# Attention steps moved into the transposed projections of a hybrid attention block, with the small projections rearranged

## The reference

```
h = RMSNorm(x) * ln_g
qa ka va za | qb ckv iq ik iw zb | qc kc vc zc | ga gb gc = columns of h @ w_in
A: 16 heads, 2 key heads, window of 2 chunks of 64, sinks, T5 bias
B: ckv = RMSNorm(ckv); score = sum_h iw_h relu(iq_h . ik) ; best 64 keys per query;
   attention over them with keys ckv @ w_uk and values ckv @ w_uv, T5 bias
C: 16 heads over all earlier chunks, relative bias
y_b = mixer_b * silu(z_b);  merged = sum_b sigmoid(g_b) * (y_b @ w_p_b)
out = RMSNorm(x + merged @ w_o) * final_g
```

## Time and profile before

| | |
|---|---|
| time, median of 3 runs | 977.41 us (976.91 to 977.55) |
| the profiled execution's own time | 976.46 us |
| its span | 974.6 us |
| PE busy | 965.2 us (99%) |
| DVE busy | 606.9 us (62%) |
| ACT busy | 473.7 us (49%) |
| granted clock of PE, mean | 0.998 |
| DMA | 190.34 MB, mean 195 GB/s |

### The profile page before, as it was taken

How to read it: one execution, slowest core, us unless ns; L and a number is a source line. 1 busy time by engine, 2 the same in 40 slices (tenths; PEclk the granted TensorE clock), 3 DMA queues, 4 the chain that set the end, 5 groups by cost and what they waited for, 6 DMA issues and landing times.

```text
span 974.6 us, 13317 instructions
## 1 busy us (share of the span) xinstructions
PE 965.2 (99%) x5136; PEld 814.8 (84%) x5136; DVE 606.9 (62%) x1129; ACT 473.7 (49%) x785; POOL 27.6 (3%) x28
## 2 busy tenths in 40 slices
PE   9999999999999999999999999999999999999996
PEld 7888888888888888888888888888888888888885
DVE  7585655676675756586765555766655555555563
ACT  7553444555453545463553544644534444444442
POOL 0030000000000110010000000000000000000000
PEclk9999999999999999999999999999999999999999
DMA  9853645465554655554654745646455677565553
GB/s 337 294 187 119 233 170 193 154 222 177 204 193 142 233 176 184 197 205 141 243 186 148 253 155 191 208 152 225 163 191 181 198 294 227 180 189 187 176 176 126
DMA packets 54766, 190.34 MB, mean 195 GB/s; under 512 B 6192, under 2 KB 7088, under 8 KB 54064
## 3 DMA queue, kind: packets, MB, share of 16 engines
q1 hardware_dynamic: 54416, 189.23, 57.1%
q10 hardware_dynamic: 288, 0.27, 0.1%
HBM read 187.38 MB, written 2.10 MB: 194 GB/s over the span
## 4 chain that ended last, share of the span: by engine, by line
PE 98%; DMA 1%; SPq 0%; ACT 0%; DVE 0%; issue 0%; ACTq 0%; POOLq 0%; POOL 0%
PE bank L1015 24%; PE bank L1005 19%; PE bank L1007 19%; PE bank L1006 19%; PE bank L1018 12%; PE bank L981 2%; PE bank L1051 2%; PE bank L1071 2%; DMA raw<-in_w_s_dram 1%; PE bank L1188 0%; PE bank L1146 0%; PE bank L1147 0%; PE bank L1145 0%; DVE w_lo L634 0%; ACT w_hi L446 0%; SPq L367 0%
## 5 line engine op out<-in xcount | busy, mean ns | idle before, releaser
L634 DVE TENSOR_TENSOR w_lo<-raw,w_hi 128x1024 fp32r<-128x1024 f32 (+1 forms) x326 | 388.0, 1213 | 174.0 <-ACT w_hi L446 173.1
L446 ACT ACTIVATE w_hi<-raw 128x1024 fp32r<-128x1024 f32 (+1 forms) x326 | 334.8, 1046 | 299.5 <-PE bank L1007 206.0
L1015 PE MATMUL bank<-hT,w_hi 128*128 128x512 f32 x960 | 300.9, 397 | 0.0
L1007 PE MATMUL bank<-w_hi,hT 128*128 128x512 f32 x600 | 233.6, 389 | 0.0
L1018 PEld LDWEIGHTS bank<-hT,w_lo 128*128 128x128 f32 x960 | 178.1, 188 | 41.1
L1005 PE MATMUL bank<-w_hi,hT 128*128 128x512 f32 x504 | 197.2, 391 | 0.0
L1006 PE MATMUL bank<-w_lo,hT 128*128 128x512 f32 x504 | 196.1, 389 | 0.0
L1018 PE MATMUL bank<-hT,w_lo 128*128 128x256 f32 x960 | 186.3, 278 | 0.0
L1015 PEld LDWEIGHTS bank<-hT,w_hi 128*128 128x128 f32 x960 | 147.6, 189 | 3.4
L1007 PEld LDWEIGHTS bank<-w_hi,hT 128*128 128x128 f32 x600 | 112.8, 188 | 23.6
L1005 PE MATMUL bank<-w_hi,ybuf 128*128 128x512 f32 x296 | 116.7, 394 | 0.2 <-DVE w_lo L634 0.2
(11 more groups left out here) (152 smaller groups left out, 534.6 us busy)
## 6 DMA issues: line engine op xcount, KB each, us to landing
raw<-in_w_s_dram SPq DMA_DIRECT2D x320, 512.0 KB, 4.4
bias_t<-in_bias_dram SPq DMA_DIRECT2D x24, 384.0 KB, 3.1
raw<-in_w_s_dram SPq DMA_DIRECT2D x8, 256.0 KB, 4.2
merged<-in_x_dram SPq DMA_DIRECT2D x2, 1024.0 KB, 9.8
big<-in_x_dram SPq DMA_DIRECT2D x1, 2048.0 KB, 9.6
out_dram<-big SPq DMA_DIRECT2D x8, 256.0 KB, 2.7
big<-in_x_t_dram SPq DMA_DIRECT2D x7, 256.0 KB, 6.7
k_b<-in_final_g_dram SPq DMA_DIRECT2D x1, 1024.0 KB, 11.6
```

The lines of the kernel that those rows point to most:

```text
L446: nc.scalar.activation(halves(g)[0], raw[:, s, 0:n], ACT.Copy).then_inc(hi_ready, 1)
L634: nc.vector.tensor_tensor(low, raw[:, s, 0:n], high.bitcast(F32), ALU.subtract).then_inc(lo_ready, 1)
L1007: ins = mm(acc, xl, wh[:, e, :], start=False, stop=kt == n_kt - 1)
L1015: mm(bank[2 * (c % 2) + n][:, :], wh[:, e, n * P:(n + 1) * P], hl_t[:, kt, :, :], start=kt == 0, stop=False)
```

## The change

The order of chunks, the slots and the lags:

```
-CHUNKS = ([("kvc", 0, 0), ("v", 0, 0), ("v", 0, 1), ("iq", 0, 0), ("ik", 0, 0)] + quarters("q", 0) + quarters("z", 0)
+CHUNKS = ([("kvc", 0, 0), ("v", 0, 0), ("v", 0, 1), ("iq", 0, 0), ("ka", 0, 0)] + quarters("q", 0)
           + [k for u in range(4) for k in (("q", 1, u), ("uk", 0, u))]
           + [("q", 2, 0), ("uv", 0, 0), ("q", 2, 1), ("uv", 0, 1), ("q", 2, 2), ("q", 2, 3)]
-          + quarters("k", 0) + quarters("z", 1)
-          + branch(0) + quarters("z", 2) + branch(1) + branch(2) + quarters("o", 0))
+          + quarters("k", 0) + quarters("z", 0) + quarters("z", 1) + quarters("z", 2)
+          + branch(0) + branch(1) + branch(2) + quarters("o", 0))
+KW = 456
+IDX_AT = (3, 6)
 def slots():
-    ...
+    for i in range(-1, 7):
+        yield i, FIRST[AT["q", 1, 0]] + 2 + 5 * (i + 1)
+    for i in range(7, 24):
+        yield i, FIRST[AT["k", 0, 0]] + 4 + (7 * (i - 7) + 1) // 2
-                bias_at[SLOT_G[2 * (p // 2) - 3] + 5 + p % 2] = p
+                bias_at[SLOT_G[2 * (p // 2) - 3] + 6 + p % 2] = p
 # ACT, attend:
+                    elif q >= 0:
+                        sc.wait_ge(pv_ready, q + 1)
+                        sc.wait_ge(scored, min(q + 2, NPAIR // 2))
+                        for p in (2 * q, 2 * q + 1):
+                            for t in range(NT):
+                                nc.scalar.activation(qT[p // 8][:, p % 8, P * t:P * (t + 1)],
+                                                     bank[4 + 2 * (p % 2) + t][:, SROW:CH], ACT.Copy, scale=0.25
+                                                     ).then_inc(o_ready, 1)
-                    p = scored_at(g - 3 - e) + e        # exponentials
+                    p = scored_at(g - 2 - e) + e
 # DVE, attend: the four products by silu are gone
-                    p = scored_at(g - 2 - e) + e        # bias and maximum
+                    p = scored_at(g - 1 - e) + e
+                        if p > 1:
+                            ve.wait_ge(o_ready, 2 * p - 2)
-                    p = scored_at(g - 4 - e) + e        # scaling
+                    p = scored_at(g - 3 - e) + e
 # DVE, silu_chunk, at the end:
+                ve.wait_ge(dve_evac, dves_before(c + 1))
+                ve.wait_ge(o_ready, 4 * (4 * b + u + 1))
+                for half in range(2):
+                    m = 2 * u + half
+                    nc.vector.tensor_tensor(qT[b][:, m, :], qT[b][:, m, :], silu[:, half, :], ALU.mult
+                                            ).then_inc(y_ready, 1)
-            rounds = {("z", 0, 0): 0, ("z", 0, 1): 1, ("z", 0, 2): 2, ("z", 0, 3): 3, ("q", 1, 1): 4, ("q", 1, 3): 5,
-                      ("q", 2, 1): 6, ("q", 2, 3): 7}
+            rounds = {("q", b, u): 4 * b + u - 4 for b in (1, 2) for u in range(4)}
```

More of the change, by code:

```diff
@@ L84, in dves_before @@
 def dves_before(c):
[L86 removed]
+    return sum(k in COPIED + SUMMED + ("iq", "z", "P") for k in KINDS[:c])
 def sums_before(c):
[L91 removed]
+    return sum(BLOCKS.get(k, 0) for k in KINDS[:c])
 def tanhs_before(c):
@@ L607, in _ @@
                     sc.wait_ge(dve_evac, dves_before(c))
-                    for n in range(4 if kind == "iq" else 2):
+                    for n in range(BLOCKS[kind]):
                         carry(c, n, HD ** -0.5 if kind == "q" else 1.0)
@@ L936, in _ @@
                         transpose_lo(7)
-                if kind == "ik":
-                    ve.wait_ge(used, FIRST[c + 1])
-                    for r in (slice(0, HD), slice(HD, P)):
-                        nc.vector.tensor_copy(ikT[r, :], bank[0][0:HD, 0:SEQ])
-                    nc.vector.tensor_copy(iwT, bank[0][HD:HD + IH, 0:SEQ]).then_inc(dve_evac, 1)
+                if kind == "ka":
+                    ve.wait_ge(carried, sums_before(c) + 1)
+                    for group in range(2):
+                        src = slice(HD * group, HD * (group + 1))
+                        for dst in (slice(0, HD), slice(HD, P)):
+                            ins = nc.vector.tensor_tensor(kT_a[dst, group, :], bank[0][src, 0:SEQ],
+                                                          gate[src, 0, SEQ:CH], ALU.add)
+                    ins.then_inc(dve_evac, 1)
                 if kind in ("v", "uv"):
                     copy_chunk(c)
-                if kind in SUMMED + ("iq",):
+                if kind in ("q", "k", "uk") + ("iq",):
                     sum_chunk(c)
@@ L999, in rows_step @@
             def rows_step(g, c, e, kt, n_kt, hi_t, lo_t, ts=range(NT)):
-                wh, wl = parts(g, CH)
+                cols = KW if KINDS[c] == "kvc" else CH
+                wh, wl = parts(g, cols)
                 for t in ts:
                     xh, xl = hi_t[:, kt, t * P:(t + 1) * P], lo_t[:, kt, t * P:(t + 1) * P]
-                    acc = bank[2 * (c % 2) + t][:, :]
+                    acc = bank[2 * (c % 2) + t][:, 0:cols]
                     mm(acc, xh, wh[:, e, :], start=kt == 0, stop=False)
@@ L1138, in _ @@
                             ins.then_inc(ckvT_ready, 1)
-                    elif kind == "ik":
-                        pe.wait_ge(lo_ready, g + 1)
-                        wh, wl = (w[:, g % RING, 0:288].rearrange("p (k n) -> p k n", k=4) for w in (w_hi, w_lo))
-                        acc = bank[2 * (c % 2)][0:72, 0:SEQ]
-                        for e in range(4):
-                            kt = 4 * j + e
-                            mm(acc, wh[:, e, :], h_hi[:, kt, :], start=kt == 0, stop=False)
-                            mm(acc, wh[:, e, :], h_lo[:, kt, :], start=False, stop=False)
-                            ins = mm(acc, wl[:, e, :], h_hi[:, kt, :], start=False, stop=kt == KT - 1)
-                        ins.then_inc(used, 1)
+                            pe.wait_ge(act_evac, 1)
+                            pe.wait_ge(dve_evac, 1)
+                            for t in range(NT):
+                                ins = transpose(bank[6][:, t * P:(t + 1) * P], ik[:, t, :])
+                            ins.then_inc(ikT_ready, 1)
                     elif kind == "uk":
```

168 lines of the change are left out of this document (66 added, 102 removed).

## The result

The changed kernel takes 1003.34 us (median of 4 runs, 1000.59 to 1006.39), beside 977.16 for the one before on the same chip: 1.027 times as long, 95% interval 1.0249 to 1.029. That is 26 us slower, and 2.3 us beyond the top of the range. The waits came as forecast; a term for TensorE's clock was missing from the sum. Its profiled execution took 1006.39 with a span of 1004.6, so it is the longest of the four.

The account below looks back on a forecast made before the run. TensorE's list bounds the kernel (99% busy). Span 974.6 - 3.3 (list) - 0.1 (end) + 15.3 (waits) + 6.4 (masks) + 1.0 (early slots) = 993.9, plus 1.9 around it: 995.8, about 995.5 us; range 986 to 1001.

Parts of the forecast that it names:

- rival 3: Long waits let TensorE's clock down behind waits of 3.1 and 5.3 us, some 1.5 each at least: 999 us, chance 0.1.
- The waits: Odd to even slots, four pieces instead of six: TensorE waits for scaled probabilities, 15.3 us over eight intervals before masks.
- S + 13.8: S is the first product behind slot 19; the walk through helper lists ends slot 20's scaling 13.8 us later, wait 2.7.
- DVE's own list: Between slots 15 and 16, VectorE's list sets the chain at 14.0 us, a wait of 2.9.
- The masks: POOL's bias masks behind slots 7, 9 and 11 hold VectorE's low parts, small sums and new product: 6.4 us, between 0 and 12.
- The list and the head: TensorE's shorter kvc, transposes and index scores save 3.3 us, between 2.6 and 4; head's wait at the eleventh piece taken as 0.
- The end: Behind the last sum, one small operation goes from POOL to DVE and the scaling is split: 0.1 us less.
- The early slots: Slots -1 and 1, five pieces to the next with uk between: waits of 0.5 us each, 1.0; slots 3 and 5 none.
- Rival 1: The waits do not come, since the lists run more closely than the walk: 973.1 us, faster; chance 0.12.
- Rival 2: The waits come, but masks fall on VectorE's idle time: 989.4 us; chance 0.2.
- Rival 4: VectorE falls behind in low parts, so pieces wait half a microsecond at each of twelve z chunks: 1001 us; chance 0.05.
- Rival 5: Waits so short that they eat the 3.4 us gained: 977 us; chance 0.03.

Follow-up runs that it names:

- filled: Changed kernel with matmuls that serve nothing ahead of the waits of seven even slots, keeping TensorE busy: 996.6 us, ratio 1.0201.
- half filled: Changed kernel with half as many matmuls that serve nothing ahead of those seven waits (7, 5, 15, 7, 7, 7, 7): 996.32 us, ratio 1.0204.
- The two shortened kernels: Changed kernel with ScalarE's carries and tanh ending z chunks, or VectorE's new product, cut from 256 to 16 columns: 1001.77 and 1000.47 us.
- VectorE's product short: Changed kernel with VectorE's new product at the end of a z chunk cut from 256 to 16 columns: 1000.47 us, one execution.
- second profile of the changed kernel: Changed kernel run again with nothing edited, for a second profile and more times: 1003.68 us, ratio 1.0272.
- measured alone: Kernel before, its order, slots and lags kept, with the changed kernel's small projections, transposes, index scores and end: 973.51 us, ratio 0.9965.
- nine profiles: Profiles of the small projections alone, the changed kernel and seven more with the same head: first transposed product began between 70.62 and 72.26.
- the last kernel: Changed kernel, odd-to-even slots six pieces apart early, five from slot 7, six between 11 and 12, two behind 12; x rows later: 973.72 us.

## Why the prediction was wrong in size and right in kind

**The step that failed is the half clock.** The sum went to 995.8 with no term for it. It stood as rival 3, with a chance of 0.1, a price of 3 us, and the sentence "Waits of 3.1 and 5.3 us reach that". That sentence took a bound from the earlier trace rows, where the clock fell some 3 us behind the last matmul, and read it as if shorter waits were safe. The runs show otherwise: waits of 2.0 to 2.8 us were followed by 1.2 GHz at slots 8, 10, 20 and 22 of the first profile. So seven waits could draw it, not two, and five did. The term is 6.7 us (1003.3 against 996.6 filled, and 996.3 half filled) where the forecast had none and the rival 3. With it the sum is 1002.5, above the range. The sum also started from the profiled execution's 976.46; the median of the kernel before is 977.16 beside the changed one, 0.7 more. The chance was wrong too: one row of a clock that falls within the length of my own waits should have put the term into the sum, or the top of the range above 1001.

**The waits.** Right: 22.7 forecast, 21.2 of idle time and 23.2 by starts; the kernels in which they are filled take 996.6 and 996.3, where the sum without clock said 995.8. Slot 18 with none, slot 12 longest, and all released by the scaling came as written. For slot 20 the walk said S + 13.8; S is 449.23 here and the scaling ended at 462.33 + 1.01 = 463.34, S + 14.1:

```profile
449.23 0.73 PE L1020 MATMUL bank<-hT,w_hi 128*128 128x512 f32 x2
```

```profile
462.33 1.01 DVE L686 TENSOR_SCALAR scores<-scores,r_denom 128x256 f32<-128x256 f32 x4
```

The two shortened kernels show whose list sets them: ScalarE's at slots 14, 20 and 22, with VectorE's product on the path of slot 20 by 0.14. Slot 16 was right as "DVE's own list", but by 0.2 only. The gap of 2.3 us or more that I had named as a sign was missed at slot 10 (2.03).

**The masks.** Forecast 6.4 (1.5, 2.3, 2.6); measured 1.1, 2.0 and 2.7, 5.7. At slot 12 POOL and VectorE of the changed kernel show the hold in both directions:

```profile
353.13 2.75 POOL L424 TENSOR_TENSOR bias_t<-bias_t,chosen 128x768 f32<-128x768 f32 x1 [5.85 <-DMA bias_t<-in_bias_dram]
```

```profile
353.00 1.23 DVE L633 TENSOR_TENSOR w_lo<-raw,w_hi 128x1024 fp32r<-128x1024 f32 x1 [0.31 <-ACT w_hi L441]
354.14 1.76 DVE L678 TENSOR_TENSOR denom<-expsum,sink_exp 128x4 f32<-128x4 f32 x1
```

The mask began inside a low part and took 2.75 instead of 1.85, while the low part kept its 1.23; the small sum behind it then took 1.76 instead of 0.15. So the mask waited for the low part, and the sum for the mask: the case that no row of before had shown. With VectorE's product short it went the other way at the first mask of this slot: in the changed kernel it had held the product (2.42 instead of 0.76 at 345.15), and now it held the low part behind it, which took 2.71 instead of 1.22:

```profile
343.27 1.85 POOL L424 TENSOR_TENSOR bias_t<-bias_t,chosen 128x768 f32<-128x768 f32 x1 [23.35 <-DMA bias_t<-in_bias_dram]
```

```profile
343.49 2.71 DVE L633 TENSOR_TENSOR w_lo<-raw,w_hi 128x1024 fp32r<-128x1024 f32 x1 [0.21 <-ACT w_hi L441]
```

The Trainium skill's rule (SBUF — State Buffer, Who interferes with whom), that whoever starts first has the shared ports to its end, agrees with these rows.

What I listed as held was incomplete. In front of slot 10 the two masks held a small sum and a scaling (L686), which reads one tile and no bank and took 2.41 instead of 1.01:

```profile
318.42 1.81 DVE L678 TENSOR_TENSOR denom<-expsum,sink_exp 128x4 f32<-128x4 f32 x1
...
320.48 2.41 DVE L686 TENSOR_SCALAR scores<-scores,r_denom 128x256 f32<-128x256 f32 x4
```

Both are on the path: VectorE has no idle time from there to the scaling that releases slot 10. Together they were held by 3.06. In the second profile of the changed kernel a low part (2.76 instead of 1.22) and the scaling (2.32) were held, by 2.85 together, and slot 10 idled 0.22 less. That the forecast of 2.3 came near is in part luck: my walk let everything on VectorE wait for the mask's end, whatever the operation.

**The list and the head.** Right in sum, 3.4 forecast and 3.36 measured alone (976.87 - 973.51). Inside it, kvc's matmuls came 0.207 apart, not 0.202: 1.9 instead of 2.4. So the other terms must have brought some 0.5 more than I gave them; no run separates them. The taking of 0 for the head's wait was 1.5 off in the profiled execution and about 0.3 off on average over nine profiles.

**The end.** 0.1 forecast, 0.1 measured. **The early slots.** 0.5 each forecast, 0.4 and 0.36 by starts.

**Behind the slots.** From the first gate product (514.41) to the last matmul (996.56) the 176 pieces took 482.2, or 2.74 each, as six of them did in 16.46 before: nothing changed there, as forecast.

**Rivals 1, 2, 4 and 5** are refuted: the waits came, the masks cost 5.7, and the only wait for a low part between slots 6 and 22 is one of 0.34. (Rival 4's twelve half microseconds on 995.8 make 1001.8, not 1001.)

## What to carry to other kernels

When an order is changed, measure the distance between two steps that depend on each other against the list that the slowest helper engine must work off between them, interval by interval; here one piece more per interval gave back 26 us with the same work in the same places. Put into the sum, and not among the rivals, what a wait does to the clock behind it: here waits of 2.0 us and more on TensorE were in some executions followed by a stretch at 1.2 GHz that lost 1.5 to 3.0 us, and it comes in one execution and not in the next, so the range has to be wide on that side. And evening out a sequence by one place can put a copy behind another engine's long item, so look at both neighbours of the interval that is widened.

## What the runs showed of the hardware that was not expected

- Equal waits, unequal clock: 2.79 us at slot 16 was followed by 1.00 in one profile (transposes 1.53) and by 0.50 in the next (2.82). Over the profiles, waits of 1.31 to 1.58 us (eight) and one of 1.81 were not followed by a lower clock; the shortest that was had 2.00. Of those from 2.0 to 2.8 us some were and some weren't.
- The runs of a kernel with such waits spread over 9 us (998.85 to 1008.12), those of the same kernel with the waits filled over 0.7.
- The loss behind one wait reached 3.0 us (6.6 us at a granted clock of 0.55 behind slot 20), more than the wait itself.
- A mask on POOL that began 0.13 us inside a low part of VectorE took 0.9 longer; one that began 0.1 ahead of it made the low part 2.83 instead of 1.22 (at 341.84 in the last kernel).
